# Reordered transfers around the sample attention and the state space layer of a two-layer decoder step

## The chip, the cores and the metric

The kernel runs on one core of one Trainium2 chip. The metric is the device time of one execution in microseconds. Five engines work from queues of their own and meet at semaphores: TensorE (PE) for matmuls and transposes into PSUM, VectorE (DVE), ScalarE (ACT), GpSimd (POOL), and SyncE (SP), which in this kernel issues every transfer. A semaphore of a transfer rises by 16 when the transfer has landed.

## The reference, cut to what matters

One inference step of a decoder with two layers, for a prompt of 1024 tokens and a sample group of 8 sequences with 8 new tokens each, in float32 and with one set of weights. Layer 0 runs two things side by side on one normalised input:

```python
z = h @ w_in_ab                        # queries, keys, values of three groups, and u
for g, (win, dil) in enumerate(((128, 1), (512, 4), (2048, 16))):
    # 8 heads of 64; the prompt in banded blocks, the sample against its cache
    o, m, l = dilated_prompt(...) if prompt else gathered_attn(...)
wts = exp(m_all - m_all.max(0))        # the three groups, combined by their denominators
out_a = sum(wts * o) / sum(wts * l)
y, h_last = s5_scan(u, ...)            # 32 groups of 16 channels, 64 complex states each
out_b = gelu(y) * sigmoid(gelu(y) @ w_glu + b_glu)
mix = concat(out_a, out_b) @ w_out_ab
```

After it come a squared-ReLU MLP (1024 to 4096 and back) and a gated per-layer embedding. Layer 1 has windowed attention with sinks in place of the two, and then the same. The caches and the states after the step are outputs too.

## The kernel before, in words

Everything is feature-major: features on the 128 partitions, 1092 columns for 64 sample tokens, 1024 prompt tokens and 4 of padding. A float32 product is made from three passes over rounded halves (high by high, low by high, high by low). The weights lie in 111 slots of 1.1 MB. SP loads a slot into `w_raw` (`feed`, L353), GpSimd splits it into a high and a low part (L645, L647) in one of two buffers, and TensorE works it off (L773, L798). SP may feed a slot when GpSimd has split the one before; GpSimd may split when TensorE has done the slot before the last. `feed_to(n)` feeds up to slot n - 1 in order.

The order of the work in layer 0 is written out by hand for each engine:

- The inputs u of the state space layer (slots 0 and 1) are stored to the DRAM area `u_turn`. VectorE and TensorE make the layer's tables, which SP parks in DRAM: `s5_ca`, `s5_b`, `s5_t` (2 to 2.3 MB each, with semaphores such as `b_parked`), and `s5_k`, a 16 x 32 x 240 array of which eight shifted windows of 128 columns make the matrix `d_mat`.
- Three prompt groups g follow. Each takes six slots (two of values, four of queries and keys), then `attend` over 8 tiles of 128 queries. A tile's output leaves from the one buffer `o_st` to the DRAM area `og` (L459 to L467), and VectorE waits for this store (`o_out`) before it writes the next tile's sums into `o_st` (L1756). In the third group SP also issues the first loads of the sample attention between the tiles: keys of samples 0 and 1 behind tiles 0 and 2, and behind tile 4 the mask and the 13 transfers of sample 0's values (`load_values`, 2.3 MB).
- The sample attention works on four pairs of samples. SP reads the new queries, keys and values back from DRAM (`qs`, `ks_new`, `vs_new`, L486 to L489, one semaphore `sx_in`), after it has waited for all stores of prompt tiles; VectorE waits for all three before it clears and fills the query tile `qb` (L1998, L2007), TensorE before its first scores (L972). For each pair there are 4.7 MB of keys and as much of values, in `kt_sb` and in `va` and `v_sb`. TensorE makes scores (L972), turns probabilities (L983, L985) and weights values (L998); ScalarE copies the result to `so` (L1408), TensorE turns it (L1003), and VectorE takes it (L1646).
- Between these, the prompt's three groups are combined in 8 tiles, two for each pair: SP loads `og_in` (L507), VectorE makes weight differences (L2053), ScalarE their exponentials (L1411), VectorE combines (L2061 to L2066) and SP stores to `mix` (L512).
- The state space layer then has its inputs loaded: `ub` in 8 loads (L534), `b_mat` (L535), and after waits for the end of the sample attention and for the last `mix` stores `ubs` in 8 loads of 16 KB (L545), `t_tab` (L546), `h0` (L547), `d_mat` in 8 loads (L549) and `ca` (L550). TensorE turns `ub` (L1021) and `ubs` (L1025), ScalarE and VectorE copy the results to `ut` (L1416, L1418, L2079), TensorE makes the states' inputs with `b_mat` (L1038) in six chunks, VectorE scans them over blocks with `t_tab` in two halves (L2088 to L2104), and TensorE makes the outputs with `d_mat` and `ca` (L1047, L1052): first the sample's four groups, then the prompt's two halves, each of which waits for its half of the scans.
- The gate slot, the output projection, the MLP and the rest follow.

Buffers share room: `ub` lies behind `v_sb` where the tables were made, `b_mat` behind the tiles of the sample attention, `d_mat` on them, `t_tab` on `vs_new`, `ks_new` and `og_in`, `ca` on `v_sb`, and `ubs` on parts of `va` and the mask.

## Time and profile before

| what | us |
|---|---|
| median of 3 runs (lowest to highest) | 3690.28 (3689.4 to 3693.12) |
| the profiled execution | 3701.41 |
| its span, first to last instruction | 3699.6 |

The span is what the profile divides into stretches; the rows of the profile all come from the one profiled execution, whose own time is 1.8 us above its span. The page gives for each engine the busy time, for 40 slices of the span the busy tenths and the granted clock of TensorE, then the DMA queues, the chain of work that ended last, and the costliest groups of instructions. A line of the timeline is the start in us, the duration in us, the engine, the line of the kernel, the operation with its output and input, the number of instructions merged, and in brackets the idle time before it with what ended it. SPq stands for an issue of a transfer by SP, and its duration reaches from the first issue of a group to the last; "issue" as a releaser means that the profile shows nothing that the engine waited for.

### The profile page before, as it was taken

What the parts mean: (1) busy time and instruction counts of PE and PEld (TensorE: products, weight loads), DVE (VectorE), ACT (ScalarE), POOL (GpSimd) and SP (SyncE); (2) the same over time, 40 slices, a digit from 0 to 9 for tenths busy, and PEclk for the clock granted to TensorE, in tenths of its full rate; (3) what the DMA queues carried; (4) which work ended last, traced back from release to release, by engine and by line L of the source; (5) the groups of instructions that cost most, each with busy time, mean ns of one, the idle gap of its engine ahead of it and who ended that gap; (6) DMA issues with size and microseconds to landing.
All of it is one profiled execution on the core that took longest, in us unless ns stands there. A gap on an engine that the chain in (4) does not pass through costs nothing.

```text
span 3699.6 us, 50510 instructions
## 1 busy us (share of the span) xinstructions
PE 3319.2 (90%) x21025; PEld 3172.0 (86%) x21025; DVE 1402.3 (38%) x1852; ACT 907.2 (25%) x1876; POOL 781.2 (21%) x226
## 2 busy tenths in 40 slices
PE   5978999994467999999999899987899999999988
PEld 4977997983357899999999899976789999999988
DVE  7704013023452443333333753165253333333364
ACT  3106125052031420000000531275142000000051
POOL 2220120210001122222222232200022222222321
PEclk9989999987688999999999999999799999999999
DMA  2221210337941122222225112100112222222411
GB/s 110 93 79 42 91 67 21 120 123 244 288 113 61 37 98 90 85 94 94 94 94 183 41 55 80 54 1 32 61 37 85 79 79 79 79 70 75 164 42 62
DMA packets 84130, 323.03 MB, mean 87 GB/s; under 512 B 19032, under 2 KB 32152, under 8 KB 66072
## 3 DMA queue, kind: packets, MB, share of 16 engines
q1 hardware_dynamic: 84000, 321.18, 25.1%
q8 instruction: 96, 1.57, 0.2%
q14 instruction: 34, 0.28, 0.0%
HBM read 271.98 MB, written 105.23 MB: 102 GB/s over the span
## 4 chain that ended last, share of the span: by engine, by line
PE 78%; DVE 8%; ACT 6%; issue 3%; DMA 2%; SPq 2%; POOL 0%; ACTq 0%; DVEq 0%
PE psum L773 60%; PE psum L798 6%; PE psum L714 2%; PE psum L845 2%; PE psum L870 2%; ACT pr L1300 1%; PE psum L748 1%; DVE stat L1790 1%; ACT pt L1308 1%; DVE xa L1713 1%; DVE sm L1785 1%; DVE rs L1660 1%; SPq L549 1%; DVE h_lo L1650 1%; DMA v_sb<-in_v 1%
## 5 line engine op out<-in xcount | busy, mean ns | idle before, releaser
L645 POOL CAST w_hi<-w_raw 128x2184 fp32r<-128x2184 f32 x109 | 224.8, 2062 | 2840.4 <-PE psum L773 2152.0
L773 PE MATMUL psum<-h_hi,w_hi 128*128 128x364 f32 x2832 | 627.9, 330 | 37.5 <-ACT xa L1258 20.9
L773 PE MATMUL psum<-h_lo,w_hi 128*128 128x364 f32 x2544 | 564.0, 330 | 5.9 <-DVE h_hi L1690 5.9
L647 POOL TENSOR_TENSOR w_lo<-w_raw,w_hi 128x2184 fp32r<-128x2184 f32 x109 | 542.4, 4976 | 8.7
L773 PEld LDWEIGHTS psum<-h_hi,w_hi 128*128 128x128 f32 x2832 | 495.0, 189 | 39.2 <-ACT xa L1258 21.2
L773 PE MATMUL psum<-h_hi,w_lo 128*128 128x364 f32 x2304 | 510.1, 330 | 0.0
L2228 DVE TENSOR_TENSOR xa<-xa,psum 128x1092 f32<-128x1092 f32 x256 | 330.7, 1292 | 382.6 <-PE psum L773 382.4
L773 PEld LDWEIGHTS psum<-h_lo,w_hi 128*128 128x128 f32 x2544 | 442.2, 189 | 6.4 <-DVE h_hi L1690 6.2
L773 PEld LDWEIGHTS psum<-h_hi,w_lo 128*128 128x128 f32 x2304 | 401.0, 189 | 0.0
L1572 ACT ACTIVATE tmp<-tmp 128x1092 f32<-128x1092 f32 x64 | 71.6, 1118 | 1255.6 <-DVE tmp L2212 1255.6
L773 PE MATMUL psum<-hid_hi,w_hi 128*128 128x364 f32 x1536 | 338.6, 328 | 5.4 <-DVE xa L2228 5.4
L773 PE MATMUL psum<-hid_lo,w_hi 128*128 128x364 f32 x1536 | 340.0, 330 | 0.0
L773 PE MATMUL psum<-hid_hi,w_lo 128*128 128x364 f32 x1536 | 339.2, 329 | 0.0
L1785 DVE TENSOR_TENSOR sm<-psum,mask 128x512 f32<-128x512 f32 (+1 forms) x160 | 94.4, 590 | 516.8 <-PE psum L845 513.5
L2212 DVE SCALAR_TENSOR_TENSOR tmp<-psum,sq 128x1092 f32<-128x1092 f32 x64 | 82.7, 1295 | 533.4 <-PE psum L773 508.8
L773 PEld LDWEIGHTS psum<-hid_hi,w_hi 128*128 128x128 f32 x1536 | 267.6, 189 | 6.0 <-DVE xa L2228 6.0
L773 PEld LDWEIGHTS psum<-hid_lo,w_hi 128*128 128x128 f32 x1536 | 267.3, 188 | 0.0
L773 PEld LDWEIGHTS psum<-hid_hi,w_lo 128*128 128x128 f32 x1536 | 266.6, 188 | 0.0
L798 PE MATMUL psum<-w_hi,h_hi 128*128 128x256 f32 x648 | 186.1, 287 | 21.8 <-DVE h_lo L1650 20.1
L798 PE MATMUL psum<-w_hi,h_lo 128*128 128x256 f32 x648 | 184.8, 285 | 0.0
L1300 ACT ACTIVATE pr<-sm,stat 128x256 f32<-128x256 f32 (+1 forms) x320 | 147.1, 460 | 94.9 <-DVE stat L1790 49.7
L798 PE MATMUL psum<-w_lo,h_hi 128*128 128x256 f32 x576 | 164.8, 286 | 0.0
(317 smaller groups left out, 4408.8 us busy)
## 6 DMA issues: line engine op xcount, KB each, us to landing
w_raw<-in_wall SPq DMA_DIRECT2D x111, 1092.0 KB, 5.0
kt_sb<-in_kt SPq DMA_DIRECT2D x16, 1024.0 KB, 10.3
out_ovs<-in_v SPq DMA_DIRECT2D x8, 2032.0 KB, 15.5
x_keep<-xa SPq DMA_DIRECT2D x2, 4368.0 KB, 11.8
xd_late<-x_keep SPq DMA_DIRECT2D x2, 4368.0 KB, 14.0
out_oks<-in_kt SPq DMA_DIRECT2D x8, 1008.0 KB, 8.3
out_ovs<-in_v SPq DMA_DIRECT2D x8, 1008.0 KB, 8.9
og<-o_st SPq DMA_DIRECT2D x24, 264.0 KB, 2.0
```

The source lines that it names most:

```text
L645: pool.tensor_copy(high[:, :], w_raw[:, :]).then_inc(hi_made, 1)
L647: pool.tensor_tensor(low[:, :], w_raw[:, :], high[:, :].bitcast(F32), ALU.subtract).then_inc(split, 1)
L714: mm = pe.matmul(UNIT[m][:, c, :], w[:, kc, m * P:m * P + P], x[:, kc, c * CH:(c + 1) * CH], start=kc == 0 and w is WH and x is XH, stop=k ...
L773: mm = pe.matmul(UNIT[s][:, c, :], w[:, kc, cols], x[:, kc, c * CH:(c + 1) * CH], start=first, stop=last)
L798: mm = pe.matmul(psum[:, 3 * s + c, 0:256], x[:, kc], w[:, kc, :], start=kc == 0 and x is XH and w is WH, stop=kc == KC - 1 and x is XL)
L845: mm = pe.matmul(psum[:, k % 2, hh * 256:hh * 256 + nk * P], staged[:, h, :], K[:, kt], start=True, stop=True)
L870: mm = pe.matmul(psum[:, 4 + h // 8, (h % 8) * HEAD_DIM:(h % 8 + 1) * HEAD_DIM], pt[:, o:o + P], vals[:, bass.ds(t, 1), c:c + HEAD_DIM], s ...
L1300: mm = act.activation(pr[:, o:o + nk * P], sm[:, o:o + nk * P], ACT.Exp, bias=stat[:, h:h + 1], accum_out=stat[:, 16 + h:17 + h])
L1572: act.activation(TMP[:, m, :], TMP[:, m, :], ACT.Square).then_inc(act_own, 1)
L1785: dve.tensor_tensor(out, psum[:, k % 2, :].rearrange("p (h c) -> p h c", h=2)[:, :, 0:nk * P], m.unsqueeze(1).broadcast_to([P, 2, nk * P]) ...
L2212: dve.scalar_tensor_tensor(chunked(TMP[:, m, :]), UNIT[m], 0.0, chunked(rs2), ALU.max, ALU.mult).then_inc(free[m], 1)
L2228: dve.tensor_tensor(chunked(XA[:, m, :]), chunked(XA[:, m, :]), UNIT[m % 2], ALU.add).then_inc(free[m % 2], 1)
```

## The change

All of it concerns when and from where things are loaded; the arithmetic is as before.

- In the second prompt group SP copies the eight windows of `s5_k` to a new DRAM area `s5_d`, laid out as `d_mat` is, with two weight feeds between them, loads `ub`, and copies the sample's inputs to a new area `us_turn`, laid out as `ubs` is. The matching loads later become one load each (`d_mat` from `s5_d`, `ubs` from `us_turn`).
- In the third prompt group the mask goes behind tile 3 and sample 0's values behind tiles 4 and 5, in halves.
- The loads of `qs` and `ks_new` don't wait for the stores of the prompt tiles any more (the wait moves ahead of the first `og_in`); `vs_new` has a semaphore of its own, for which TensorE waits ahead of the weighted values; VectorE clears `qb` ahead of its wait.
- `b_mat` is loaded ahead of the last two combinations. `ubs`, `t_tab` and `h0` are issued ahead of the waits for the last taken outputs and the `mix` stores, `d_mat` and `ca` behind them.
- TensorE's wait for the last taken outputs moves from ahead of the `ub` transposes to the fourth chunk of L1038, the first that uses their PSUM bank.
- In the last pair ScalarE makes the two combinations' exponentials ahead of the copy to `so`.

```diff
@@ SP, second prompt group @@
+                elif g == 1:
+                    sp.wait_ge(k_parked, 16)
+                    sp.wait_ge(kz_in, 16)
+                    for k in range(L_BLK):
+                        sp.dma_start(s5_d[16 * k:16 * k + 16, :, :], s5_k[:, :, 16 * k:16 * k + P]).then_inc(d_spread, 16)
+                        if k in (2, 5):
+                            feed_to(first + 6 + k // 3)
+                    sp.wait_ge(u_out, 32)
+                    sp.wait_ge(t_parked, 16)
+                    for k in range(L_BLK):
+                        src = u_turn[SAMPLE:SAMPLE + SEQ, :].rearrange("(b s) c -> s b c", s=L_BLK)[L_BLK - 1 - k]
+                        sp.dma_start(UB[:, k, :], src).then_inc(ub_in, 16)
+                        src = u_turn[0:SAMPLE, :].rearrange("(n s) c -> s n c", s=NS)[NS - 1 - k]
+                        sp.dma_start(us_turn.rearrange("n (s c) -> s n c", s=L_BLK)[k], src).then_inc(us_spread, 16)
                 units.skip(2, 2, 2, 2)
...
@@ SP, third prompt group and first queries @@
-                        elif t == 4:
+                        elif t == 3:
                             load_mask(0)
-                            load_values(0, 0)
+                        elif t >= 4 and t < 6:
+                            load_values(0, 0, (range(2), range(2, 4))[t - 4])
                 sp.wait_ge(out_done, stored.at)
             sp.wait_ge(kept, keeps.at)
-            sp.wait_ge(o_out, oout.at)
             sp.wait_ge(pv_mm, N_A_STEPS)
...
-            sp.dma_start(vs_new[0:SAMPLE, :], v_keep.rearrange("t g c -> t (g c)")).then_inc(sx_in, 16)
+            sp.dma_start(vs_new[0:SAMPLE, :], v_keep.rearrange("t g c -> t (g c)")).then_inc(vs_in, 16)
...
+            sp.wait_ge(o_out, oout.at)
             load_outputs(0)
@@ SP, last pair and state space layer @@
                 if z < 3:
                     next_values(z + 1)
+                else:
+                    sp.wait_ge(b_parked, 16)
+                    sp.dma_start(b_mat[:, :], s5_b).then_inc(bm_in, 16)
                 mixed(2 * z)
                 mixed(2 * z + 1)
-            sp.wait_ge(u_out, 32)
-            for parked in (ca_parked, b_parked, k_parked, t_parked):
-                sp.wait_ge(parked, 16)
-            sp.wait_ge(kz_in, 16)
-            for k in range(L_BLK):
-                src = u_turn[SAMPLE:SAMPLE + SEQ, :].rearrange("(b s) c -> s b c", s=L_BLK)[L_BLK - 1 - k]
-                sp.dma_start(UB[:, k, :], src).then_inc(ub_in, 16)
-            sp.dma_start(b_mat[:, :], s5_b).then_inc(bm_in, 16)
+            sp.wait_ge(ca_parked, 16)
             sp.wait_ge(kv_used, 8)
             sp.wait_ge(ss_norm, 4)
+            sp.wait_ge(us_spread, 16 * L_BLK)
+            sp.dma_start(ubs[0:NB, :], us_turn).then_inc(ubs_in, 16)
+            sp.dma_start(t_tab[:, :], s5_t).then_inc(t_in, 16)
+            sp.dma_start(h0[:, :], a["h0"]).then_inc(h0_in, 16)
             sp.wait_ge(spv_taken, 4)
             sp.wait_ge(mix_out[0], 64)
             sp.wait_ge(mix_out[1], 64)
-            for k in range(L_BLK):
-                src = u_turn[0:SAMPLE, :].rearrange("(n s) c -> s n c", s=NS)[NS - 1 - k]
-                sp.dma_start(UBS[0:NB, k, :], src).then_inc(ubs_in, 16)
-            sp.dma_start(t_tab[:, :], s5_t).then_inc(t_in, 16)
-            sp.dma_start(h0[:, :], a["h0"]).then_inc(h0_in, 16)
-            for k in range(L_BLK):
-                sp.dma_start(DM[16 * k:16 * k + 16, :, :], s5_k[:, :, 16 * k:16 * k + P]).then_inc(d_in, 16)
+            sp.wait_ge(d_spread, 16 * L_BLK)
+            sp.dma_start(d_mat[:, :], s5_d.rearrange("p g k -> p (g k)")).then_inc(d_in, 16)
             sp.dma_start(ca[:, :], s5_ca).then_inc(ca_in, 16)
@@ TensorE @@
             def pair_outputs():
                 pe.wait_ge(spv_taken, spt_.add() - 1)
+                pe.wait_ge(vs_in, 16)
...
-            pe.wait_ge(spv_taken, 4)
             pe.wait_ge(ub_in, 16 * L_BLK)
...
             for i, (j0, n) in enumerate(V_CHUNKS):
+                if i == 3:
+                    pe.wait_ge(spv_taken, 4)
@@ ScalarE, each pair z @@
-                act.wait_ge(kv_used, kvu.add(2))
-                act.activation(so[:, :], psum[:, 6, 0:256], ACT.Copy).then_inc(so_made, 1)
+                if z < 3:
+                    outputs_out()
                 for b in range(2):
                     act.wait_ge(w_dif, n_sc.add())
                     act.activation(c_w[:, b * 64 + 32:b * 64 + 56], c_w[:, b * 64 + 8:b * 64 + 32], ACT.Exp).then_inc(w_exp, 1)
+                if z == 3:
+                    outputs_out()
@@ VectorE @@
-            dve.wait_ge(sx_in, 48)
             dve.wait_ge(pv_mm, N_A_STEPS)
             step(dve.memset(qb[:, :], 0.0))
+            dve.wait_ge(sx_in, 32)
```

`outputs_out` holds the two removed lines of ScalarE.

## Rows read from the trace of the kernel before

**Rows 1.** The page's head: span and instructions.

```profile
span 3699.6 us, 50510 instructions
```

**Rows 2.** Busy time by stretch: us, per engine busy (instructions), PEclk, DMA share, GB/s.

```profile
740.00:925.00 185.00, 131.26 (x1029) 112.37 (x1031) 56.52 (x149) 72.65 (x241) 13.72 (x4) 0.77 0.57 184
925.00:1110.00 185.00, 105.48 (x1330) 79.54 (x1322) 87.72 (x179) 39.24 (x64) 0.00 (x0) 0.76 0.69 200
```

**Rows 3.** Timeline of VectorE, end of the third prompt group: start, us, operation.

```profile
845.12 0.17 DVE L1756 COPY o_st<-stat 128x8 f32<-128x8 f32 x1 [4.68 <-DMA og<-o_st]
...
855.75 0.69 DVE L1770 TENSOR_TENSOR o_st<-psum,stat 128x512 f32<-128x512 f32 x1 [2.04 <-PE psum L870]
```

**Rows 4.** Timeline of all engines, first queries of the sample attention.

```profile
858.65 0.56 SPq L486 DMA_DIRECT2D qs<-qk_keep  x1
...
866.83 0.70 DVE L1998 MEMSET qb<- 128x768 f32 x1 [10.39 <-DMA vs_new<-v_keep]
...
868.87 1.51 PE L972 MATMUL psum<-ks_new,qb 128*32 128x64 f32 x48 [13.22 <-DVE qb L2007]
```

**Rows 5.** Busy time by stretch, the sample attention as a whole.

```profile
854.00:996.00 142.00, 70.72 (x1207) 49.32 (x1210) 52.60 (x131) 14.44 (x30) 0.00 (x0) 0.71 0.95 299
```

**Rows 6.** Timeline of all engines, last combinations to the second half's outputs.

```profile
994.11 0.17 DVE L1832 TENSOR_TENSOR c_w<-og_in 128x8 f32<-128x8 f32 x1 [8.54 <-DMA og_in<-og]
...
996.89 0.21 ACT L1411 ACTIVATE c_w<-c_w 128x24 f32<-128x24 f32 x1
...
1006.79 0.86 DVE L1646 TENSOR_SCALAR oas<-psum 64x32 f32<-64x32 f32 x4
...
1015.61 25.82 SPq L549 DMA_DIRECT2D d_mat<-s_k  x8
...
1017.03 6.65 PE L1021 MATMUL psum<-ident,ub 128*128 128x128 f32 x32 [19.55 <-DMA ub<-u_turn]
...
1024.83 3.69 PE L1025 MATMUL psum<-ident,ubs 8*128 8x8 f32 x32 [1.15 <-DMA ubs<-u_turn]
...
1029.04 9.71 PE L1038 MATMUL psum<-ut,b_mat 128*64 128x136 f32 x128 [0.52 <-issue]
...
1035.87 1.23 DVE L2088 TENSOR_TENSOR rx<-hv,t_tab 128x1024 f32<-128x1024 f32 x1 [11.40 <-ACT hv L1423]
...
1054.69 1.01 PE L1047 MATMUL psum<-d_mat,ut 128*8 128x128 f32 x4 [15.93 <-issue]
...
1075.35 0.29 DVE L2112 TENSOR_TENSOR sx<-h,s5k 128x128 f32<-128x128 f32 x1
...
1089.05 0.68 PE L1047 MATMUL psum<-d_mat,ut 128*128 128x128 f32 x4 [0.69 <-ACT zb L1442]
```

**Rows 7.** Timeline of SP and GpSimd, second prompt group.

```profile
448.44 1.26 SPq L431 DMA_DIRECT2D v_sb<-v_turn  x2
...
468.03 48.26 SPq L353 DMA_DIRECT2D w_raw<-in_wall  x3
...
484.85 2.01 POOL L645 CAST w_hi<-w_raw 128x2184 fp32r<-128x2184 f32 x1 [17.00 <-PE psum L773]
```

**Rows 8.** DMA issues: operation xcount, KB each, median us from issue to landing.

```profile
w_raw<-in_wall SPq DMA_DIRECT2D x111, 1092.0 KB, 5.0
...
ca<-s_ca SPq DMA_DIRECT2D x1, 2304.0 KB, 13.1
...
ks_new<-qk_keep SPq DMA_DIRECT2D x1, 384.0 KB, 5.3
...
ys<-ys_turn SPq DMA_DIRECT2D x1, 128.0 KB, 2.4
```

**Rows 9.** Busy time by stretch, the state space layer.

```profile
1025.00:1045.00 20.00, 13.24 (x160) 12.91 (x160) 8.99 (x12) 5.40 (x13) 0.00 (x0) 0.79 0.99 144
...
1054.60:1060.40 5.80, 5.71 (x37) 2.29 (x37) 5.73 (x6) 0.00 (x0) 0.00 (x0) 0.50 0.01 3
1060.40:1074.60 14.20, 14.09 (x158) 7.38 (x156) 13.99 (x25) 3.25 (x7) 0.00 (x0) 0.99 0.01 1
```

More of the change, by code:

```diff
@@ L120, in build @@
     s5_k = nc.dram_tensor("s5_k", (16, 32, 15 * 16), F32).ap()
+    s5_d = nc.dram_tensor("s5_d", (P, 32, P), F32).ap()
+    us_turn = nc.dram_tensor("us_turn", (NB, NS * 512), F32).ap()
     mix = nc.dram_tensor("mix", (SEQ, 512), F32).ap()
@@ L390, in load_keys, with load_values @@
                     o += c
-            def load_values(n, b):
+            def load_values(n, b, parts=range(4)):
                 vb = (va, v_sb)[b]
-                sp.dma_start(vb[:, 0:512], a["v"][0][bass.ds(n, 1), :, :].rearrange("n p c -> p (n c)")).then_inc(v_in[b], 16)
-                for c in range(4):
+                if 0 in parts:
+                    sp.dma_start(vb[:, 0:512], a["v"][0][bass.ds(n, 1), :, :].rearrange("n p c -> p (n c)")).then_inc(v_in[b], 16)
+                for c in parts:
                     sp.dma_start(vb[:, 512 * (1 + c):512 * (2 + c)],
@@ L437, in _ @@
                     sp.dma_start(s5_ca, ca_e[:, :]).then_inc(ca_parked, 16)
-                    feed_to(first + 6)
                     sp.wait_ge(b_evict, 8)
@@ L1022, in _ @@
                 mm.then_inc(ut_mm, 1)
-            pe.wait_ge(ubs_in, 16 * L_BLK)
+            pe.wait_ge(ubs_in, 16)
             for g in range(32):
@@ L1054, in block_outputs @@
                 return mm
-            pe.wait_ge(d_in, 16 * L_BLK)
+            pe.wait_ge(d_in, 16)
             pe.wait_ge(ca_in, 16)
@@ L1406, in _, with outputs_out @@
                     pair_exp()
-                act.wait_ge(kv_used, kvu.add(2))
-                act.activation(so[:, :], psum[:, 6, 0:256], ACT.Copy).then_inc(so_made, 1)
+                def outputs_out():
+                    act.wait_ge(kv_used, kvu.add(2))
+                    act.activation(so[:, :], psum[:, 6, 0:256], ACT.Copy).then_inc(so_made, 1)
+                if z < 3:
+                    outputs_out()
                 for b in range(2):
```

7 lines of the change are left out of this document (4 added, 3 removed).

## The prediction

> **What bounds the kernel now.** I read the page's head first: the profiled span is 3699.6 us [rows 1], one core, so no other core matters. The busy times by stretch come next: between 740 and 1110 us TensorE works 131.26 and then 105.48 of 185 us, at mean granted clocks of 0.77 and 0.76, while the DMA share is 0.57 and 0.69 [rows 2]. That is the stretch which the change aims at, and in it TensorE waits for data. The chain of waits names whom it waits for, and the timeline gives the times. Three places are to be seen there. At the end of the third prompt group VectorE idles 4.68 us before it may overwrite the output tile, because the tile's store is behind a sample's values in the DMA queue; the last tile is done at 855.75 + 0.69 = 856.44 [rows 3]. Then the first queries: the three small loads that start the sample attention are issued only at 858.65, when the last store has landed, VectorE waits for the last of the three, and TensorE's first scores start at 868.87 [rows 4]. From there to 996 us the DMA share is 0.95 at 299 GB/s, so the transfer engines set the pace [rows 5]. Last, the state space layer: after the sample attention its inputs are fetched in one queue. TensorE turns the prompt inputs at 1017.03, the sample inputs at 1024.83, starts the state matmuls at 1029.04, and then idles 15.93 us until 1054.69, when the last of the eight d_mat loads and the load of ca are in; the issue of the eight alone held SP for 25.82 us [rows 6].
>
> **The change part by part**, in the order of time, on the time axis of before.
>
> Second prompt group (added work). Eight copies of 512-byte pieces inside DRAM, eight loads of ub and eight copies for the sample inputs now stand in SP's queue between the feeds of the weights. What could wait is the feed: SP has its queue free from 448.44 + 1.26 = 449.70, and three feeds run from 468.03 over 48.26 us, about 24 us apart. GpSimd takes up the first of them at 484.85 [rows 7]; with 5.0 us to land [rows 8] a feed has 484.85 - 468.03 - 5.0 = 11.8 us to spare. The eight d_mat loads, the same 512-byte pieces but into SBUF, held SP for 25.82 / 8 = 3.2 us each [rows 6]. Three of them are 10 us in an 18 us gap, so I cost this at nothing, covered by those gaps. Bounds: nothing, and twice 3.2 us, as both ends are in DRAM, with 1.5 us for each of the others (256 KB at the 370 KB a us that I work out below are 0.7, doubled likewise): 8 x 6.4 + 16 x 1.5 = 75 us in the 78 us from 449.70 to the last feed's latest useful time (468.03 + 48.26 + 11.8 = 528.1), still next to nothing. Without that cover every microsecond of a late feed is paid.
>
> Values of the first sample in two halves, the mask a tile earlier. The queue in front of a tile's store is halved, and a tile lies between the halves. I take the whole 4.68 us [rows 3]; bounds 0 and 4.68.
>
> First queries. SP no longer waits for the last store: the queries go out about 0.65 us behind it instead of 858.65 - 856.44 = 2.21, so 1.6 us earlier. VectorE clears its tile ahead of the wait and needs only the keys, which are issued 0.6 us after the queries and take 5.3 us [rows 8]: 857.1 + 0.6 + 5.3 = 863.0. From the end of the clear to the scores was 868.87 - 867.53 = 1.34 us [rows 4], so the scores start near 864.3, 4.5 us earlier, and with the 4.68 us 9.2 us.
>
> Sample attention. Little of the second step survives here: at a DMA share of 0.95 [rows 5] the phase ends when its bytes are in, and the bulk (the second sample's values, right behind the three small loads) starts 4.7 + 1.6 = 6.3 us earlier. I take 6.3; the bounds are 0 and 9.2. b_mat joins that queue behind the last outputs and lands in the idle time after it.
>
> The last two combinations. Their exponentials no longer stand behind the copy that waits for the last values on ScalarE. In before VectorE was ready at 994.11 + 0.6 = 994.7 and the exponential came at 996.89, 2.0 us later than it could [rows 6]. So VectorE gets to the last outputs at 1006.79 - 6.3 - 2.0 = 998.5 and is through at 999.4. In return TensorE gets the copy that it turns last only behind the second exponential. One combination is half of 1006.79 - 996.89, 5 us, so that is at 996.89 - 8.3 + 5 = 993.6, and with copy and turn 994.5; VectorE is later than that anyway.
>
> State space layer. ub has long been in, so its 32 transposes (6.65 us) start at about 995; half of their copies are on VectorE and wait for 999.4, so they end near 1002.5. The sample inputs are now one load of 128 KB, issued near 999.2; a load of that size took 2.4 us [rows 8], so it is in at about 1001.6. Then 3.69 us of transposes and about 0.5 us of copy: the state matmuls start at 1006.8 instead of 1029.04 [rows 6], 22.2 us earlier. VectorE's scans follow 1035.87 - 1029.04 = 6.8 us later, at 1013.6, and take 1075.35 - 1035.87 = 39.5 us, to 1053.1.
> For the three large loads (t_tab, d_mat, ca) I estimate a rate from two rows: 1092 KB in 5.0 us and 128 KB in 2.4 us [rows 8] leave 964 KB for 2.6 us, 370 KB a us. t_tab (2048 KB), issued at 999.7, is in at 999.7 + 2.4 + 1920 / 370 = 1007.3, ahead of the scans. d_mat, now one contiguous load, waits only for the last mix store, so it queues right behind: 2048 / 370 = 5.5 us, 1012.8. ca: 2304 / 370 = 6.2 us, 1019. The end for slow transfers is the pace of before: 144 GB/s with the d_mat pieces in flight [rows 9] and 13.1 us for ca [rows 8], so d_mat at 1007.3 + 14.6 and ca at 1035. I take the quick end, since the loads are contiguous like the weights in the 5.0 us row.
> The sample outputs thus start at 1019, not 1054.69. The second half's outputs started at 1089.05, 34.4 us later, which gives 1053.4; moreover the clock was at 0.50 (1.2 GHz) for the first 5.8 us after the idle stretch and at 0.99 (2.4 GHz) after it [rows 9], and with the idle stretch shrunk to about 2 us I expect the 2.9 us back: 1050.5. The scans end at 1053.1, so they decide: **1053.3 for 1089.05, 35.7 us**. What follows (gate, output projection) is a chain of the same steps, and carries the gain to the end.
>
> The added waits cost nothing by these times: TensorE's for vs_new comes only ahead of the first weighted values, after the next pair's scores, its wait ahead of the fourth chunk near 1011 is for the 999.4 of VectorE, and SP's two are for copies of the second prompt group.
>
> **Sum.** The profiled execution took 3701.4 us, its span 3699.6 and 1.8 around it. 3701.4 - 35.7 = 3665.7. The median of the runs shown, 3690.28, is 11.1 us below that execution, so I forecast 3654.6, rounded 3655.
>
> **A rule against the change.** In before, the stretch of the d_mat loads moved 144 GB/s at a DMA share of 0.99 [rows 9], and I blame their 512-byte pieces. The Trainium skill, "DMA: Bandwidth & Descriptors", section Specifications, puts the smallest transfer for line rate at 512 B. By that rule the pieces are no fault and the rearranged area gains nothing in transfer; the trace speaks against it, though what else was in that queue could be to blame.
>
> **Rivals.**
> 1. The rate stays low for another reason than the size of the pieces. Then d_mat's 2.1 MB take 14.6 us at 144 GB/s, 9.1 more than taken: ca is in at 1028, the second half starts at 1062.5, the gain is 26.5: 3664. For it: the loads were queued together, so the rows don't separate them. Against it: the weights' 5.0 us. Chance 0.14. (It is where the rule of the Trainium skill, "DMA: Bandwidth & Descriptors", Specifications, would lead.)
> 2. The sample attention keeps its end: the bytes are the same, and the keys of the next pair wait for scores, so 6.3 us could go into gaps. 35.7 - 6.3 = 29.4: 3661. For it: the phase's share of 0.95, not more. Against it: its first load moves as a whole. Chance 0.12.
> 3. Slower: the DRAM copies hold up the weights of the second group. The place is SP's queue; the price is what the third feed is late beyond 11.8 us. It cancels the gain when that feed is 35.7 + 11.8 = 47.5 us late, at 516.3 + 47.5 = 563.8: 114 us for the 24 transfers, of which the other 16 take some 24, so 11 us for each of the eight copies, 3.5 times the 3.2 us of before. At 13 us each it is 8 x 13 + 24 - 114 = 14 us slower than now: 3704. Against it: the gaps of [rows 7]. Chance 0.03.
> 4. The change does not shorten the path, because something unseen (the order of landing in one queue) makes TensorE wait for ca as long as before: 3690. Chance 0.03.
>
> **How the numbers follow.** My forecast has 0.68. Its own ends are the full 9.2 us in the sample attention (38.6 us: 3652) and t_tab or ca 5 us late (3660), with some 3 us for the clock: 3648 to 3661. The range reaches to rivals 1 and 2 and a part of the slow end: 3648 to 3669. A measurement of this kernel tells about 0.2%, 7.4 us, from no change. Faster by more than that: the forecast, rivals 1 and 2, 0.94; within it 0.03; slower 0.03.
>
> **What would show it.** Right: no wait of VectorE for the tile's store; the first scores about 8 us after the last prompt tile rather than 12.4; the state matmuls 16 to 17 us after the last values' matmuls, not 32; the wait ahead of the sample outputs at 2 to 3 us; a second half that starts on VectorE's scans. Wrong step by step: GpSimd waiting for weights near 485 to 540; DMA share below 0.95 inside the sample attention; a rate near 144 GB/s after it. The prediction is wrong if the outputs of the second half move by less than 21 us.

## The result, and the profile after

The changed kernel took 3632.39 us (median of 4, 3631.19 to 3641.45) where the kernel before, measured beside it, took 3689.84: a ratio of 0.9845 (95% interval 0.9823 to 0.9867), 57 us less. The forecast was 3655, its range 3648 to 3669. The direction was right, and the gain was larger than the range allows. In a second measurement (e17) five more executions had a median of 3641.09, ratio 0.986 (0.9833 to 0.9887), 52 us less. That median is outside the range too; only the upper end of its interval, 3649 us, touches it.

The profiled execution took 3641.45 us, the slowest of the four. Its span answers to [rows 1]:

```profile
span 3639.6 us, 50510 instructions
```

That is 60.0 us less, between two executions that were 9 and 11 us above their medians. The gain comes from two places 600 us apart, and the prediction looked at one of them.

**The first prompt group, which the prediction didn't look at.** The timeline of the kernel before, first prompt group, engines SP, GpSimd, ScalarE and TensorE (columns as in [rows 3]):

```profile
162.70 0.33 SPq L437 DMA_DIRECT2D s_ca<-ca_e  x1
...
196.95 2.00 POOL L645 CAST w_hi<-w_raw 128x2184 fp32r<-128x2184 f32 x1 [34.84 <-PE psum L773]
...
203.84 0.33 SPq L353 DMA_DIRECT2D w_raw<-in_wall  x1
204.37 0.33 SPq L440 DMA_DIRECT2D s_b<-bm_e  x1
204.75 0.64 SPq L442 DMA_DIRECT2D s_k<-bt  x1
216.63 2.05 ACT L1258 ACTIVATE xa<-psum 128x1092 f32 x2 [55.89 <-DMA s_k<-bt]
217.76 1.28 PE L773 MATMUL psum<-h_hi,w_hi 128*128 128x364 f32 x3 [20.88 <-ACT xa L1258]
...
243.51 2.01 POOL L645 CAST w_hi<-w_raw 128x2184 fp32r<-128x2184 f32 x1 [39.70 <-PE psum L773]
```

SP parks s5_ca at 162.70 and then stands in a weight feed until 203.84. That feed may go only when GpSimd has split the slot before, and GpSimd starts on it only when TensorE has finished a slot, at 196.95. Only behind the feed does SP issue the stores of s5_b and s5_k. ScalarE waits for both (L1379, L1380) before it takes the first queries and keys out of PSUM, and TensorE, which waits for ScalarE to free its PSUM, idles 20.88 us. The same stretch of the changed kernel:

```profile
162.40 0.33 SPq L441 DMA_DIRECT2D s_ca<-ca_e  x1
162.78 0.42 SPq L443 DMA_DIRECT2D s_b<-bm_e  x1
175.18 0.66 SPq L445 DMA_DIRECT2D s_k<-bt  x1
184.71 1.08 ACT L1271 ACTIVATE xa<-psum 128x1092 f32 x1 [24.29 <-PE psum L784]
196.62 2.01 POOL L656 CAST w_hi<-w_raw 128x2184 fp32r<-128x2184 f32 x1 [34.81 <-PE psum L784]
...
203.77 0.34 SPq L356 DMA_DIRECT2D w_raw<-in_wall  x1
...
220.59 2.01 POOL L656 CAST w_hi<-w_raw 128x2184 fp32r<-128x2184 f32 x1 [16.99 <-PE psum L784]
```

The store of s5_k is issued 29.6 us earlier, ScalarE waits for TensorE's sums and no longer for a store, and TensorE does not stop. The two kernels differ in one line for this, which the section on the change and its diff leave out and the prediction never mentions (first prompt group, SP):

```diff
                     sp.dma_start(s5_ca, ca_e[:, :]).then_inc(ca_parked, 16)
-                    feed_to(first + 6)
                     sp.wait_ge(b_evict, 8)
```

The slot is fed by the call that follows the store of s5_k. GpSimd's next split comes 22.9 us earlier than before (220.59 against 243.51).

**First queries and sample attention**, timeline of the changed kernel, answering to [rows 3] and [rows 4]:

```profile
820.46 0.17 DVE L1776 COPY o_st<-stat 128x8 f32<-128x8 f32 x1 [1.19 <-DMA og<-o_st]
...
823.09 0.69 DVE L1790 TENSOR_TENSOR o_st<-psum,stat 128x512 f32<-128x512 f32 x1 [2.28 <-PE psum L881]
823.88 0.70 DVE L2017 MEMSET qb<- 128x768 f32 x1
824.27 0.56 SPq L503 DMA_DIRECT2D qs<-qk_keep  x1
...
831.77 1.05 DVE L2027 TENSOR_SCALAR qb<-qs 64x96 f32<-64x96 f32 x4 [7.19 <-DMA ks_new<-qk_keep]
...
833.07 1.51 PE L983 MATMUL psum<-ks_new,qb 128*32 128x64 f32 x48 [10.09 <-DVE qb L2027]
```

VectorE's wait for the tile's store is 1.19 us instead of 4.68; the query tile is cleared while the queries are being issued, ahead of the wait for them; the scores start 9.3 us after the last tile (833.07 - 823.78) instead of 12.4, where about 8 were forecast. In the stretch from there on, busy time as in [rows 5], the DMA share is 0.99 instead of 0.95:

```profile
824.00:962.00 138.00, 68.39 (x1194) 47.07 (x1198) 51.29 (x127) 14.06 (x29) 0.00 (x0) 0.71 0.99 307
```

**State space layer**, timeline of the changed kernel, answering to [rows 6]:

```profile
962.07 0.17 DVE L1852 TENSOR_TENSOR c_w<-og_in 128x8 f32<-128x8 f32 x1 [9.64 <-DMA og_in<-og]
...
962.68 0.22 ACT L1429 ACTIVATE c_w<-c_w 128x24 f32<-128x24 f32 x1 [14.03 <-DVE c_w L2073]
...
972.59 0.86 DVE L1666 TENSOR_SCALAR oas<-psum 64x32 f32<-64x32 f32 x4
973.08 0.30 SPq L553 DMA_DIRECT2D ubs<-us_turn  x1
...
974.70 0.32 SPq L560 DMA_DIRECT2D d_mat<-s_d  x1
...
977.35 3.69 PE L1036 MATMUL psum<-ident,ubs 8*128 8x8 f32 x32 [1.51 <-DMA ubs<-us_turn]
...
981.57 9.48 PE L1051 MATMUL psum<-ut,b_mat 128*64 128x136 f32 x128 [0.52 <-issue]
...
988.16 1.23 DVE L2108 TENSOR_TENSOR rx<-hv,t_tab 128x1024 f32<-128x1024 f32 x1 [11.53 <-ACT hv L1443]
...
994.15 0.60 PE L1060 MATMUL psum<-d_mat,ut 128*8 128x128 f32 x4 [3.10 <-issue]
...
1027.66 0.71 PE L1060 MATMUL psum<-d_mat,ut 128*128 128x128 f32 x4 [0.97 <-DVE hv L2124]
```

The wait ahead of the sample outputs is 3.10 us instead of 15.93, and the second half now starts on VectorE's scans (hv), as forecast. ScalarE's exponential (962.68) now follows VectorE at once. Counted from the end of the last values' matmuls, the state matmuls come 19.0 us later instead of 32.5; 16 to 17 were forecast. The loads behind it, from the list of transfers (answering to [rows 8]: KB, then us from issue to landing), and the two stretches in which they ran (answering to [rows 9]):

```profile
ca<-s_ca SPq DMA_DIRECT2D x1, 2304.0 KB, 19.0
...
t_tab<-s_t SPq DMA_DIRECT2D x1, 2048.0 KB, 8.5
d_mat<-s_d SPq DMA_DIRECT2D x1, 2048.0 KB, 13.9
...
ks_new<-qk_keep SPq DMA_DIRECT2D x1, 384.0 KB, 6.8
```

```profile
980.00:985.00 5.00, 4.48 (x41) 4.42 (x42) 0.00 (x0) 0.74 (x2) 0.00 (x0) 0.50 1.00 423
985.00:990.00 5.00, 5.00 (x87) 5.00 (x85) 1.84 (x2) 3.07 (x8) 0.00 (x0) 0.96 1.02 431
```

With the same DMA share of about 1.0, 423 and 431 GB/s are moved where [rows 9] had 144.

### The profile page after: what moved, and what is told of

Its sections match the earlier page's. It is cut to its first block, busy times and chain, and to the rows that moved or that the text cites. A ratio compares the mean times of both kernels' runs of the same rounds, so it can differ in the third digit from the quotient of the medians.

```text
span 3639.6 us, 50510 instructions
## 1 busy us (share of the span) xinstructions
PE 3310.4 (91%) x21025; PEld 3163.5 (87%) x21025; DVE 1402.4 (39%) x1852; ACT 907.6 (25%) x1876; POOL 779.6 (21%) x226
## 4 chain that ended last, share of the span: by engine, by line
PE 79%; DVE 9%; ACT 6%; issue 3%; DMA 2%; SPq 1%; ACTq 0%; DVEq 0%
PE psum L784 61%; PE psum L809 6%; PE psum L856 2%; PE psum L725 2%; PE psum L881 2%; ACT pr L1313 1%; PE psum L759 1%; DVE stat L1810 1%; ACT pt L1321 1%; DVE xa L1733 1%; DVE sm L1805 1%; DVE rs L1680 1%; DVE h_lo L1670 1%; DVE xa L1741 1%; PE psum L983 1%
## 5 line engine op out<-in xcount | busy, mean ns | idle before, releaser
L1313 ACT ACTIVATE pr<-sm,stat 128x256 f32<-128x256 f32 (+1 forms) x320 | 147.1, 460 | 90.4 <-DVE stat L1810 45.3
## 6 DMA issues: line engine op xcount, KB each, us to landing
xd_late<-x_keep SPq DMA_DIRECT2D x2, 4368.0 KB, 13.9
```

What stands on the lines that cost most here:

```text
L1313: mm = act.activation(pr[:, o:o + nk * P], sm[:, o:o + nk * P], ACT.Exp, bias=stat[:, h:h + 1], accum_out=stat[:, 16 + h:17 + h])
```

## The experiments

All times are medians; "gain" is the ratio's distance from 1, times 3690, with its interval. Where a time can't separate two cases, the table below does: one profiled execution of each kernel, all times in us counted from the same event, GpSimd's split of the last weight slot of the third prompt group (775.57 in the kernel before), so that what came earlier drops out. All columns are starts: of the first scores, of the last block of weighted values, of the state matmuls, of the sample's outputs, and of the outputs of the prompt's second half. One trace stands for a kernel, and traces with the same edits ahead of a column differ by some us: in the fourteen with all edits of the first queries, the last values lie between 210.0 and 218.2. Next weights is GpSimd's first split after the state space layer (1153.6 before).

| kernel | first scores | last values | state matmuls | sample outputs | second half | next weights |
|---|---|---|---|---|---|---|
| before | 93.3 | 217.5 | 253.5 | 279.1 | 313.5 | 378.0 |
| feed alone (e1 / e16) | 90.8 / 91.9 | 214.6 / 216.7 | 249.0 / 252.9 | 271.9 / 276.7 | 305.0 / 310.2 | 368.0 / 373.8 |
| first queries alone (e3) | 85.2 | 210.5 | 245.5 | 269.2 | 303.2 | 367.4 |
| state space alone (e4), with feed (e15) | 91.8 / 92.3 | 217.7 / 216.0 | 237.9 / 237.0 | 250.5 / 249.6 | 284.9 / 282.9 | 350.0 / 347.0 |
| feed put back (e2) | 83.9 | 218.2 | 238.4 | 251.0 | 285.4 | 348.1 |
| changed (first / e17) | 84.9 / 84.5 | 212.2 / 210.6 | 233.4 / 231.4 | 246.0 / 244.0 | 279.5 / 278.5 | 343.9 / 341.3 |
| pieces (e5) | 83.4 | 214.3 | 235.5 | 260.5 | 294.2 | 358.0 |
| eight loads, 16 partitions (e6) | 85.7 | 214.5 | 235.1 | 259.7 | 293.4 | 357.2 |
| eight loads, 128 partitions (e13) | 84.1 | 211.8 | 233.0 | 245.7 | 279.3 | 343.9 |
| one load, small pieces (e14) | 83.1 | 211.1 | 232.3 | 245.4 | 278.6 | 343.0 |
| so first (e7) | 83.3 | 210.0 | 233.2 | 245.7 | 279.5 | 344.0 |
| b_mat late (e8) | 84.9 | 212.4 | 239.4 | 252.0 | 286.2 | 358.4 |
| values whole (e9) | 88.7 | 217.1 | 238.0 | 250.5 | 283.8 | 347.8 |
| copies twice (e10) | 84.0 | 210.7 | 232.3 | 244.8 | 278.7 | 344.1 |
| ca early (e11) | 83.5 | 211.5 | 231.2 | 242.0 | 276.8 | 347.4 |
| inputs early (e12 / e18) | 83.5 / 84.5 | 210.8 / 213.0 | 226.9 / 228.9 | 240.4 / 242.2 | 274.9 / 276.6 | 339.6 / 347.3 |

### The feed of the first prompt group (e1, e16, e2)

Edit of e1 and e16: the kernel before with the one removed line shown above, and nothing else. Edit of e2: the changed kernel with that line put back.

e1: 

> Before, with one line of the change alone: in the first prompt group SP no longer feeds weight slots 6 and 7 between the parking of s5_ca and the loading of s5_b's area. Theory (the part of the gain that the prediction missed comes from this line): before stood 20.9 us at TensorE from 196.9 us, because SP waited in that feed until 203.8 us and issued the parking of s5_b and s5_k only then, so that ScalarE's work behind s_k came 32 us later than in the changed kernel. The wait goes and TensorE starts its next matmuls at 185 to 197 us; the whole run is 23 to 27 us shorter, about 3664 us. Rival A (the whole unforecast gain comes from the sample attention and the state space layer, and the stall moves to the next feed): no change, about 3690. Rival B (the line is worth its stall alone, and the clock gives nothing back): 20 to 22 us, about 3669.

e16: 

> The kernel before without the one feed, once more, since its runs spread from 3659 to 3683 us where others spread over 10. If the feed is worth 23 us and more whatever follows: a median of 3663 to 3668. If it is worth 17 us: 3670 to 3675, and the profile shows a stretch after the second prompt group that gives back what the first had gained, at a lower granted clock.

e2: 

> The changed kernel with that one feed put back ahead of the parking of s5_b. Theory: the stall of TensorE at 197 us comes back, and the run is 23 to 27 us longer than the changed kernel, 3656 to 3660, which is what the prediction worked out for the rest of the change (3655), within 1 to 5 us. Rival A (the line is worth nothing): 3632. Rival B (with the copies of the second prompt group in SP's queue the late feeds now also delay that group): more than 30 us longer, above 3663.

Measured: e1 3672.84, ratio 0.9953 (0.9938 to 0.9968), a gain of 17 us (12 to 23); e16 3668.81, 0.9935 (0.9921 to 0.9949), 24 (19 to 29). e2 3660.62, 0.9914 (0.9897 to 0.993): the rest of the change gains 32 (26 to 38). The timeline of e16 shows the mechanism alone:

```profile
162.68 0.42 SPq L439 DMA_DIRECT2D s_b<-bm_e  x1
175.09 0.64 SPq L441 DMA_DIRECT2D s_k<-bt  x1
184.64 1.08 ACT L1257 ACTIVATE xa<-psum 128x1092 f32 x1 [24.31 <-PE psum L772]
```

and that of e2 has the stall back:

```profile
205.60 0.65 SPq L446 DMA_DIRECT2D s_k<-bt  x1
217.42 2.05 ACT L1272 ACTIVATE xa<-psum 128x1092 f32 x2 [55.84 <-DMA s_k<-bt]
218.56 1.28 PE L785 MATMUL psum<-h_hi,w_hi 128*128 128x364 f32 x3 [20.84 <-ACT xa L1272]
```

The line is the missing term: the rival that gave it nothing is out in both directions. e1 came out below both of its figures, with an interval that reaches them, and e16 between its two cases. No stretch gives the gain back in e16. In e2 the second prompt group adds nothing to the stall: GpSimd's splits there stay 24 us apart. The size is harder: by the times it is 17 (e1), 24 (e16), 18 (e15 less e4) and 20 to 25 (the changed kernel less e2), and e1's executions spread from 3659 to 3683. The traces are closer. At the place itself, from GpSimd's split near 197 us to its next, the four traces with the feed (the kernel before, e2, e3 and e4) took 46.6 to 47.8 us and the sixteen without it 24.0: 22.6 to 23.8 us, with no overlap. At the last split of the third group, the sixteen stand on average 28.8 us ahead of the kernel before, and the four (the kernel before among them) 5.5: 23.3 us.

### The two parts that the prediction did cover (e3, e4, e15)

Edits: e3 is the kernel before with the edits of the third prompt group and the first queries; e4 is the changed kernel without these, and with the feed put back; e15 is e4 without the feed. Nothing else differs from the diff shown.

e3: 

> Before, with the edits around the first queries alone: the values of sample 0 in halves, the mask a tile earlier, the queries and keys not behind the stores of the prompt tiles, a semaphore of its own for the new values, the query tile cleared ahead of its wait. Theory: the first scores come 8.4 us earlier (to 860.5 us on the axis of before), and what is left of it at the end of the sample attention is 4.6 us, since that stretch ends when its bytes are in: 3684 to 3686. Rival (all of the 8.4 us reach the end): about 3681. Rival (the last loads of the state space layer take it all): 3690.

e4: 

> The changed kernel with the feed put back and the edits around the first queries undone: what is left is the state space layer's part (rearranged areas, order of its loads, ScalarE's order in the last pair). Theory: 35.7 us were forecast for both parts and 6.3 of them for the first queries; 34.0 and 4.6 were seen in the traces, so this part alone gives 28 to 30 us against before: about 3661. Rival (the parts overlap, since both pull the same loads ahead, and one alone gives almost all): 33 us or more, 3657 or less. If the first queries' edits only matter together with it: below 26 us, 3664 or more.

e15: 

> The changed kernel with the edits around the first queries undone, the feed of the first prompt group left out as in the change. By the sum of parts: 3690 less 25.8 for the state space layer (measured alone) less the feed. If the feed is worth 25 us in company: 3639 to 3641. If it is worth 17 us: 3646 to 3649.

Measured: e3 3684.06, ratio 0.9973 (0.9959 to 0.9988), a gain of 10 us (4 to 15). e4 3665.34, 0.993 (0.9913 to 0.9946), 26 (20 to 32). e15 3647.52, 0.988 (0.9865 to 0.9896), 44 (38 to 50), which is the case of a feed worth 17 us. e4 gained a little less than the theory's 28 to 30, which lie within its interval. By its figure alone it falls to the expectation's last case (3664 or more: the first queries' edits only matter together with it); against that case stand e3's 10 us, gained without it. The parts add up within their intervals: 10 + 26 against the 32 of e2, which has both. In the table the second half comes at 309.6 on average without either part (before, e1, e16), 303.2 with the first, 283.9 with the second (e4, e15), 279.0 with both (changed, e17). e2, which has both too, stands at 285.4 in a profiled execution that took 8 us more than its median; with it the mean for both is 281.1.

### Why the loads of d_mat were slow (e5, e6, e13, e14)

Edits, each in the changed kernel: e5 loads d_mat as before, in pieces of 512 bytes out of s5_k, and makes no copies; the other three keep the copies, and in e14 they lay s5_d out by group (32 x 128 x 128).

```diff
 e6
-            sp.dma_start(d_mat[:, :], s5_d.rearrange("p g k -> p (g k)")).then_inc(d_in, 16)
+            for k in range(L_BLK):
+                sp.dma_start(DM[16 * k:16 * k + 16, :, :], s5_d[16 * k:16 * k + 16, :, :]).then_inc(d_in, 16)
 e13
+            for k in range(L_BLK):
+                sp.dma_start(DM[:, 4 * k:4 * k + 4, :], s5_d[:, 4 * k:4 * k + 4, :]).then_inc(d_in, 16)
 e14
+            sp.dma_start(DM[:, :, :], s5_d.rearrange("g p k -> p g k")).then_inc(d_in, 16)
```

e5: 

> The changed kernel with d_mat loaded in eight loads of 512-byte pieces out of s5_k, at the new place in the queue, and without the copies to s5_d in the second prompt group. Theory (the pieces made the transfers of before slow, the prediction's reason): SP is held for about 20 to 26 us by the eight loads, the rate of the stretch falls from 335 GB/s to about 150 to 200, ca lands 9 to 15 us later, and the second half's outputs, which wait for the scans, come about 6 to 10 us later: 3638 to 3643. Rival (512 bytes are enough for the full rate, the Trainium skill's DMA: Bandwidth & Descriptors, section Specifications; the order of the queue did the rest): no change, 3632, with d_mat in 14 us after its issue as in the changed kernel.

e6: 

> The changed kernel with the load of d_mat from the rearranged area s5_d split into eight loads of 16 partitions each, whole rows of 16 KB. It tells the size of the pieces from the number of loads. Theory of the pieces: 0 to 1 us longer (3632 to 3633), each issue of SP well below 1 us. Rival (eight loads are slow because there are eight, each on few partitions): SP is held about as long as by the pieces and the time is that of the kernel with pieces.

e13: 

> The changed kernel with the load of d_mat from s5_d in eight loads again, but each over all 128 partitions and an eighth of the columns (2 KB pieces). It tells the number of loads from the number of partitions that a load fills. Theory A (a load that fills 16 partitions is slow, whatever its pieces; the eight of e6 moved 125 to 149 GB/s): no change against the changed kernel, 3632 to 3641, sample outputs 11 to 14 us after the state matmuls start. Theory B (eight loads are slow because there are eight): as e6, about 3650, sample outputs 24 us after the state matmuls start.

e14: 

> The changed kernel with s5_d laid out by group instead of by row, so that d_mat is still one load over 128 partitions, but in pieces of 512 bytes. It tests the size of the pieces by itself. Theory A (the partitions decide, and 512 bytes are enough, as the Trainium skill's DMA: Bandwidth & Descriptors, section Specifications, has it): 3632 to 3641. Theory of the pieces (the prediction's reason): sample outputs later by 5 to 14 us, 3640 to 3650.

Measured: e5 3650.66, ratio 0.9893 (0.9876 to 0.9909); e6 3650.37, 0.9895 (0.9878 to 0.9911); e13 3640.27, 0.9857 (0.9842 to 0.9872); e14 3639.93, 0.9858 (0.9843 to 0.9873). e5 and e6 had one chip, e13 and e14 another, so the ratios are to be compared: 0.9845 and 0.986 for the changed kernel. Between the start of the state matmuls and the sample outputs lie 25.0 us in e5, 24.6 in e6, but 12.7 in e13 and 13.1 in e14 (changed 12.6). Busy time by stretch, e6, with whole rows of 16 KB to 16 partitions a load:

```profile
985.00:990.00 5.00, 5.00 (x86) 5.00 (x85) 2.54 (x3) 3.09 (x8) 0.00 (x0) 0.97 1.01 125
990.00:995.00 5.00, 0.31 (x6) 0.06 (x2) 4.90 (x5) 1.02 (x3) 0.00 (x0) 1.00 1.04 134
```

and e13, as many loads, each to all 128 partitions:

```profile
985.00:990.00 5.00, 5.00 (x63) 5.00 (x61) 0.00 (x0) 1.85 (x5) 0.00 (x0) 0.68 1.12 439
990.00:995.00 5.00, 3.65 (x64) 3.39 (x60) 4.17 (x4) 3.17 (x8) 0.00 (x0) 1.00 0.86 366
```

e14's list of transfers gives its pieces, 0.5 KB, and its landing, as quick as the 13.9 us of the whole rows:

```profile
d_mat<-s_d SPq DMA_DIRECT2D x1, 0.5 KB, 14.3
```

So neither the pieces (e14) nor the number of loads (e13) is at fault. A load that fills 16 partitions is slow whatever its pieces: 125 to 134 GB/s against 366 to 439, with the 16 DMA engines about as busy (in the second stretch of e13 ca is on its way too). The landing says the same of d_mat alone: the median of the eight loads is 17.0 us after the issue in e6 and 8.7 in e13. The theory of the pieces is wrong, and e6's expectation of no change with it. e6's rival was right on the time and wrong on SP, which the eight issues held for 3.73 us, against 14.36 in e5. What small pieces do cost is SP's time: behind the one load of e14, SP's issue of ca took 9.44 us, against 0.48 in the changed kernel; ca landed after 19.0 us in both. The Trainium skill, "SBUF — State Buffer", section "Door 1: The DMA port swizzle", states this rule: partitions 0 to 15 reach 4 of 16 ports, measured there at 104 GB/s for 1 MiB, against 328 for all 128. The runs agree in kind, at 125 to 134 here. The rule that the prediction weighed, the Trainium skill's "DMA: Bandwidth & Descriptors", section Specifications, by which 512 bytes are enough, also agrees with e14.

That e5 cost more than its 6 to 10 us has a plain reason: the sample outputs are 14.5 us later, so TensorE and not VectorE's scans sets the second half's start (294.2 against 279.5).

### Smaller terms (e7 to e10)

e7 puts ScalarE's copy to so ahead of the exponentials in the last pair too; e8 loads b_mat behind the last two combinations; e9 issues the mask and all of sample 0's values behind tile 4; e10 makes each copy to s5_d twice.

```diff
 e7
-                if z < 3:
-                    outputs_out()
+                outputs_out()
 e9
-                        elif t == 3:
+                        elif t == 4:
                             load_mask(0)
-                        elif t >= 4 and t < 6:
-                            load_values(0, 0, (range(2), range(2, 4))[t - 4])
+                            load_values(0, 0)
 e10
                         sp.dma_start(s5_d[16 * k:16 * k + 16, :, :], s5_k[:, :, 16 * k:16 * k + P]).then_inc(d_spread, 16)
+                        sp.dma_start(s5_d2[16 * k:16 * k + 16, :, :], s5_k[:, :, 16 * k:16 * k + P]).then_inc(d_spread2, 16)
```

e7: 

> The changed kernel with ScalarE's copy to so ahead of the last two exponentials again, as in before. Theory: the last combinations wait for the last values' matmuls again, the outputs are taken 2.0 to 2.2 us later, and as the state space layer hangs on them and ends on the scans, the run is about 2 us longer: 3634 to 3635. Rival (ub's turns have cover enough): 3632.

e8: 

> The changed kernel with b_mat loaded behind the last two combinations, ahead of the sample's inputs, as the order of before has it. Theory: the load stands in front of ubs, t_tab, d_mat and ca in the queue; 2.2 MB at the 335 GB/s of that stretch are 6.5 us, so ubs lands and the state matmuls start 5 to 7 us later and so does the end: 3637 to 3639. Rival (the sample attention ends earlier by the same amount, since b_mat's bytes are out of its queue, and gives it back): 3632 to 3634.

e9: 

> The changed kernel with the mask and the whole of sample 0's values behind tile 4 of the third prompt group again. Theory: VectorE waits 4 to 5 us for the tile's store again and the last tile is done about 3.5 us later than in the changed kernel (1.19 us of the wait are left there); of this 2 to 3 us reach the end, as the sample attention that follows is bound by its transfers, of which the values are then a larger part already in: 3634 to 3636. Rival (the transfers bind throughout, and the wait of VectorE costs nothing): 3632. Rival (all of it is paid): 3636 or more.

e10: 

> The changed kernel with each of the eight copies from s5_k to s5_d done twice, the second time into an area that nothing reads. It doubles the suspected cost of the added transfers. Theory (they are hidden in the gaps between the feeds of the second prompt group): no change, 3631 to 3634, and GpSimd's casts of that group stay about 24 us apart. Rival (the copies already cost something, which the gain hides): longer by what one set costs, up to 10 us.

Measured: e7 3638.03, ratio 0.9856 (0.984 to 0.9872), which can't be told from the changed kernel; in the trace the state matmuls come 23.2 us behind the last values instead of 21.2 (20.8 in e17), so the 2 us are there, and are too few to show in the time of a whole run. VectorE waits 2.11 us for the first exponential in e7, against 0.29 in the changed kernel. Most of that hangs on the pace of the last values: their last block took 3.80 us in this trace and 2.17 in the changed kernel's, so by estimate 0.5 us of the wait would be left at the changed kernel's pace.

e8 3649.09, 0.9888 (0.9872 to 0.9905). The state matmuls come 6 us later (27.0 behind the last values), as expected, and the second half 6.7 later; the last values come no earlier (212.4), so the rival is out. Then the way to the next weights takes 72.2 us instead of 64.4. In this profiled execution, the slowest of the four, the first 16 us of the second half ran at a granted clock of 0.50, after TensorE had waited 3.16 us for the scans. That goes with the rest of the loss in this trace; the other executions have no profile.

e9 3640.54, 0.9871 (0.985 to 0.9892). The time does not tell it from e10 on the same chip (3642.26). In the trace VectorE waits 3.86 us for a store, and the first scores (88.7) come 3 us or more behind every trace with the halves (83.1 to 85.7). Last values (217.1) and second half (283.8) are some 5 us behind the changed kernel, but e2, which has the halves, has 218.2 and 285.4 there. So the wait is shown, and how much of it reaches the end is not.

e10 3642.26, 0.9865 (0.9846 to 0.9885). The time missed the expected 3631 to 3634, as the changed kernel's own second measurement (3641.09) does. The copies lie ahead of the table's event, so the table can't show their cost; the event itself comes no later, at 747.10 us of the span against 748.13 in the changed kernel and 748.58 in e17. GpSimd's splits of the second group stay 23.97 us apart, each released by TensorE, as in the changed kernel. So the copies are hidden, as the prediction said.

### Going further (e11, e12, e17, e18)

Edits in the changed kernel: e11 and e12 load ubs and ca right behind b_mat, ahead of the last combinations. In e12 (and e18, the same kernel) TensorE moreover turns ub right behind the last weighted values, and ScalarE alone copies the results, six between its two last exponentials and two behind. e17 is the changed kernel itself.

```diff
+                    sp.dma_start(ubs[0:NB, :], us_turn).then_inc(ubs_in, 16)
+                    sp.dma_start(ca[:, :], s5_ca).then_inc(ca_in, 16)
                 mixed(2 * z)
                 mixed(2 * z + 1)
...
-            sp.dma_start(ubs[0:NB, :], us_turn).then_inc(ubs_in, 16)
             sp.dma_start(t_tab[:, :], s5_t).then_inc(t_in, 16)
...
-            sp.dma_start(ca[:, :], s5_ca).then_inc(ca_in, 16)
```

e11: 

> A version that goes further: the sample's inputs (ubs) and ca are loaded ahead of the last two combinations, behind b_mat, so that t_tab and d_mat alone are left behind them. Theory: ubs is in when TensorE has turned ub and the wait for it goes; the sample outputs no longer wait for ca, and the scans bind: 1 to 3 us shorter, about 3630. Rival (the early loads stand in front of the last og_in loads in the queue and delay the combinations by 2.3 MB at about 335 GB/s, 7 us): slower, 3635 to 3639.

e12: 

> The kernel with ubs and ca early, and besides TensorE turns ub right behind the last weighted values while ScalarE alone copies the results, between and behind its last two exponentials; VectorE's copies go. Theory: the turns no longer stand behind VectorE's last combination, the state matmuls start about 5 us earlier, and the run is 4 to 8 us shorter than the changed kernel, about 3626. Rival (eight copies on ScalarE delay the second exponential and so the last combination): no gain or up to 4 us longer than the kernel with ubs and ca early.

e17: 

> The changed kernel itself once more, beside the version with early inputs. 3632 to 3641 us, a ratio of 0.984 to 0.987; in the profile the state matmuls 20 to 21 us after the last values' matmuls and the second half's outputs on VectorE's scans, as in the first one.

e18: 

> The version with early inputs once more, on the same chip as the changed kernel. Theory (the 5 us that its trace shows at the start of the second half's outputs reach the end): 4 to 6 us below the changed kernel in the same call. Rival (the clock takes it back): within 2 us of it.

Measured: e11 3641.05, ratio 0.9864 (0.9847 to 0.9881); e12 3635.54, 0.9857 (0.9839 to 0.9874); e17 3641.09, 0.986 (0.9833 to 0.9887), and on its chip e18 3639.1, 0.9847 (0.9822 to 0.9872). None can be told from the changed kernel, so the shorter times expected of e11 and e12 did not show; e18 lies 2.0 us below e17 by the medians, the edge of its rival, and the intervals are too wide to decide. All three reach the second half 2 to 5 us earlier in their traces. In e11 and e18 the granted clock then fell, and the lead is gone at the next weights; in e12, where it stayed at 1.00, the lead is still there at the next weights (339.6), but its four executions spread from 3632 to 3641. TensorE ahead of the second half, e11, timeline, and the 16 us after it, busy time by stretch:

```profile
1025.30 0.71 PE L1060 MATMUL psum<-d_mat,ut 128*128 128x128 f32 x4 [3.64 <-DVE hv L2124]
```

```profile
1025.30:1041.30 16.00, 16.00 (x92) 12.95 (x94) 1.99 (x10) 1.80 (x3) 0.00 (x0) 0.57 0.04 10
```

The same 16 us of the changed kernel, where TensorE had waited 0.97 us:

```profile
1027.70:1043.70 16.00, 12.44 (x112) 10.04 (x112) 1.95 (x10) 9.94 (x9) 0.00 (x0) 0.99 0.30 101
```

e11 gets through 92 matmuls in the time of 112, as the clock is at its lower level (1.2 of 2.4 GHz) for most of it; in e18 it was 0.56 over the first 10 us. e11's rival, a delay of the last combinations, did not come: the last values stand at 211.5 and the state matmuls at 231.2. A version faster than both was not found; whether the early inputs would win with the clock held stays open.

## Why the prediction was wrong

**The step that failed is the list of what the change does.** "The change part by part" begins at the second prompt group. The removed feed in the first was overlooked, a term of 23 us. It was there to be read, in the chain of waits of the kernel before (start, length, link):

```profile
203.84 0.33 SPq L353
...
204.37 0.33 SPq L440
...
204.75 11.53 DMA s_k<-bt
```

The feed and the two stores behind it are links of the chain, ahead of a stall of 20.88 us. But the prediction went from the busy times straight to 740 us, "the stretch which the change aims at". Without that line (e2) the measured 3660.62 lies within the range, 6 us above the forecast.

**Second prompt group, cost nothing:** right, shown by the splits 24 us apart in the changed kernel and in e10. Rival 3 fell with it.

**First queries, 9.2 us:** right in mechanism. Over the fourteen traces with the edits (all but e9) the scores start 7.8 us earlier than in the five without. In the profile, 1.19 us of VectorE's wait stayed and ks_new took 6.8 us where 5.3 were taken.

**Sample attention, 6.3 us:** over the same traces the last values come 4.2 us earlier, so a third of the step was missing; rival 2 went too far in the other direction. The DMA share of the stretch is 0.99, but no run shows where this third went.

**Last combinations, 2.0 us:** right in mechanism, and in size at the pace that the last values had before (e7).

**State space layer.** From the last values to the second half's outputs the kernel before took 96.0 us and the changed one 67.3, a step of 28.7, where the terms gave 29.4 (35.7 less 6.3). Times of landing were taken at 7.6 us for t_tab, 13.1 for d_mat and 19.3 for ca (from the issue), and were 8.5, 13.9 and 19.0. The sample's inputs took 4.2 us, not 2.4, behind b_mat in the queue. The scans set the second half, as forecast. But one execution stood for the kernel before: in e1, e3 and e16, which have its loads, the same stretch took 90.4, 92.7 and 93.5. So 2.5 to 5.6 us of the 28.7 seem to be that execution's own, and the closeness to 29.4 is in part luck. The second half's outputs as a whole moved by 34.0 us (313.5 to 279.5), well above the 21 us below which the prediction called itself wrong.

**The reason for the quick loads was wrong, and the sum came out right all the same.** The 512-byte pieces cost the landing nothing (e14); the eight loads filled 16 partitions each (e6, e13). Rival 1 asked whether the rate stays low "for another reason than the size of the pieces". There was another reason, but the change removes it together with the pieces. So this term was right by luck.

Altogether: 23.3 from the feed, and 309.6 - 279.0 = 30.6 at the second half from the rest (28.5 with e2 among the traces with both), 54 us (52). The two measurements of the changed kernel are 57 (49 to 65) and 52 (42 to 62).

## What to carry to other kernels

Go through every hunk of a diff, one by one, and look up the wait it touches, also where the hunk is a single removed line far from the rest; in a queue that is worked in order, a feed that isn't urgent can hold a store on which two engines depend. Before blaming the size of a transfer's pieces, count the partitions that it fills. And measure stretches from a common event over several executions: one execution of the kernel before was 3 to 6 us slower in one stretch than three kernels with the same loads.

## What was not expected of the hardware

The rate of a load hung on the partitions that it fills: 125 to 134 GB/s at 16 partitions, 366 to 439 at 128, and 512-byte pieces made no difference to it.

A short wait of TensorE can be followed by a loss longer than itself. Ahead of the second half of the outputs, sixteen of the twenty profiled executions waited 0.69 to 2.69 us and kept the granted clock at 1.00 over the next 10 us; they then took 62.7 to 65.1 us to the next weights. e10 waited 2.93 us (clock 0.71 over the first 10 us, 65.4 us), e8 3.16 (0.50, 72.2) and e11 3.64 (0.58, 70.6). The length of the wait isn't all of it, since e18 fell to 0.56 after 1.79 us (70.7), while e4 kept 1.00 after 1.90. What decides between such cases stays open.
